# Two chained network blocks in one kernel: mixer ends worked off in batches, fused mask-and-maximum, and neighbourhood attention with its rotation, value transposes and bias mask placed inside its projections

## The chip, the cores and the metric

The kernel runs on one core of a Trainium2 chip. The metric is the device time of one execution in microseconds (us), here the median of three. Five engines work side by side, each through its own queue of instructions in order, and wait for one another on semaphores: PE (TensorE: matrix products, with PEld its weight loads), ACT (ScalarE), DVE (VectorE), POOL (GpSimd) and SP (SyncE, which here only issues DMAs). PSUM has eight banks of 512 fp32 values per partition.

## The reference, cut to what matters

A first block of two layers (half-step SwiGLU, a mixer, half-step SwiGLU, each with a post-norm modulated by "ada" vectors) over 256 latent and 256 context rows of width 1024. The mixer of its layer 0 is neighbourhood attention (NA), that of layer 1 a short convolution. A second block of two layers over 384 rows, of which the kernel carries 272; each layer has three mixers whose outputs are normalised per head, gated and summed:

```python
# NA (once): per head, 256 queries against 256 window keys and 256 context keys
q = apply_axial_rope(qkv[:, :, 0]); k = apply_axial_rope(qkv[:, :, 1])
s_win = where(mask, q @ k * scale + bias, -inf);  s_ctx = q @ k_c * scale
p = softmax(concatenate([s_win, s_ctx]))
out = p[..., :nk] @ v + p[..., nk:] @ v_c
# second block, per layer
o_ret = rms(retention(...)) * silu(gate)        # 4 heads of 256 columns
o_hg  = rms(hgrn2(...)) * silu(gate)            # 8 heads of 128
p = softmax(where(allowed, s, MASK_VALUE)); w = p[:, :, 0] - lam * p[:, :, 1]
o_da  = rms(w @ v) * subln_g * (1 - lambda_init) # 8 heads of 128, two score maps each
y = sum_n sigmoid(gate_n) * (branch_n @ w_branch_n)
```

## The kernel before

**GEMMs.** Everything is fp32. A weight product is made of three matrix products of reduced operands: high by high (line 1721), activation-low by weight-high (1722) and activation-high by weight-low (1723). The list `gemm_steps` gives the order of all projections. A step is worked in units of 256 output columns (two PSUM banks), a unit in chunks of K = 512: 24 matmuls per chunk. Per chunk SP fetches the raw weights (2 x 256 KB, line 1567), ACT casts them to `high` (line 1791) and DVE subtracts to get `low` (line 1969); raw, high and low have four slots. In the first block, chunks also host "ada" parts: 256 KB more of weights (L1572) and matmuls at line 1634.

**NA.** The steps are q (256 rows: 8 chunks), k and v (512 rows each: 8 chunks each), then the output projection "res". Between v's last matmul and the first scores `na_pe` transposes the values (L1377; ACT copies them, L1432), and rotates q and k: PE multiplies by a permutation (L1384), POOL multiplies by cosines (L1503), DVE by sines (L1468) and adds (L1471). DVE adds the column mask to the whole bias table `TB` (L1462) ahead of that. Then 32 units (16 heads x 2 query tiles, two units per step j) run as a pipeline: scores (PE, L1396); bias add, context copy, negated maximum (DVE, L1486, L1487, L1489); exponential with sum (ACT, L1447); reciprocal (DVE, L1478); scaling (POOL, L1506); transposes (PE, L1417); copy of them (ACT, L1443); values (PE, L1406). The score tiles `SB` are a ring of six. DVE waits for the transposes of unit t-6 before it writes unit t.

**Mixer ends.** In all three mixers of the second block (ret, hg and da; `out_bank`, `tail_act_square` to `tail_dve_low` at lines 630 to 687, and the same for hg at 1100 to 1186 and 1346 to 1356) a head's output stays in its PSUM bank through the whole chain: ACT squares it, PE sums the squares with a matrix of ones, ACT takes Ln and Exp(-0.5 x) of the sum, DVE scales and gates it out of PSUM, ACT casts, DVE subtracts. Ln and Exp are in different tables of ACT, so each alternation loads two tables. Two tiles of `SX`, `SY` and rdev alternate. The next matrix work in the program, the "mgate" step, has its first four chunks placed among the heads ("early" chunks, lines 1669 to 1671); the "branch" step follows. PE waits for the last scaled head (`s_ot`) before it goes on. In da 24 units (8 heads x 3 chunks of queries) are a pipeline over PE, DVE, ACT, with two maps each; DVE adds the mask (L986) and reduces to the maximum (L989).

The order of the work is the order in which the code of each engine is written; there is no scheduler.

## Time and profile before

| | us |
|---|---|
| median of 3 runs | 3321.48 (3318.24 to 3323.4) |
| the profiled execution's own time | 3321.1 |
| its span | 3319.3 |
| PE busy | 3015.6 (91%) |
| DVE busy | 1769.4 (53%) |
| ACT busy | 1427.5 (43%) |
| POOL busy | 431.8 (13%) |
| mean granted TensorE clock | 0.937 |

The profile is one execution. The time differs from the span by what lies outside it, 1.8 us. A matmul's busy time is modelled, so neighbouring ones overlap in the rows; the distance of their starts tells what one costs. A waiting engine appears as idle time before an instruction with the instruction that released it. Clock 1.00 is full speed; DMA share is the mean busy share of the 16 DMA engines.

### The profile page before, as it was taken

To read this page: it belongs to the slowest core of one execution; us is meant where nothing else is said; L and a number is where in the kernel's file an instruction comes from. 1 tells how busy PE (TensorE), PEld (TensorE's weight loads), DVE (VectorE), ACT (ScalarE), POOL (GpSimd) and SP (SyncE) were. 2 spreads that over 40 slices of the span, in tenths; PEclk is the share of its full clock that TensorE was granted. 3 is DMA by queue.
4 is the path that set the end of the run, shared out by engine and by line. 5 is a ranking of instruction groups with operands and counts; after the bars stand their busy time and mean duration, and the time that the engine had idled before them with its cause. 6 is when DMAs were issued, how large, how long until landed. Compare 5 with 4: busy or idle time off the path is not lost.

```text
span 3319.3 us, 53884 instructions
## 1 busy us (share of the span) xinstructions
PE 3015.6 (91%) x20792; PEld 2696.5 (81%) x20792; DVE 1769.4 (53%) x2514; ACT 1427.5 (43%) x1986; POOL 431.8 (13%) x330
## 2 busy tenths in 40 slices
PE   5999997977998989897999889889989987988898
PEld 2667765746998989897999778689988986967898
DVE  2323224375555556554547646658654574575684
ACT  1222113135445444544455443746535444355563
POOL 2111000052211101110100202001110020010110
PEclk7999998989999999998999879689999997978999
DMA  8885455601655645554445034045543530523453
GB/s 290 280 256 159 129 163 164 191 20 58 183 178 146 181 149 178 146 180 138 153 129 167 23 108 134 26 131 168 179 142 116 168 100 26 165 64 102 133 174 124
DMA packets 586160, 474.86 MB, mean 143 GB/s; under 512 B 28720, under 2 KB 547888, under 8 KB 585664
## 3 DMA queue, kind: packets, MB, share of 16 engines
q1 hardware_dynamic: 584464, 460.44, 45.2%
q0 software_dynamic: 1520, 11.95, 1.2%
q8 instruction: 125, 2.05, 0.3%
q14 instruction: 51, 0.42, 0.0%
HBM read 471.23 MB, written 4.72 MB: 143 GB/s over the span
## 4 chain that ended last, share of the span: by engine, by line
PE 83%; DVE 7%; ACT 4%; issue 3%; DMA 1%; SPq 1%; POOL 0%; DVEq 0%; ACTq 0%
PE PS L1721 24%; PE PS L1722 23%; PE PS L1723 23%; PE PS L1634 3%; PE PS L520 1%; PE PS L882 1%; PE PS L1108 1%; PE PS L870 1%; SPq L1572 1%; PE PS L1669 1%; PE PS L1670 1%; PE PS L1671 1%; ACT high L1791 1%; PE PS L718 1%; PE PS L1058 1%
## 5 line engine op out<-in xcount | busy, mean ns | idle before, releaser
L1969 DVE TENSOR_TENSOR low<-raw,high 128x1024 fp32r<-128x1024 f32 (+1 forms) x744 | 909.9, 1226 | 906.1 <-ACT high L1791 899.1
L1791 ACT CAST high<-raw 128x1024 fp32r<-128x1024 f32 (+1 forms) x744 | 767.6, 1033 | 1141.7 <-PE PS L1723 854.0
L1721 PE MATMUL PS<-NHh,high 128*128 128x272 f32 x2304 | 682.6, 296 | 65.7 <-issue 21.9
L1723 PE MATMUL PS<-NHh,low 128*128 128x272 f32 x2304 | 674.8, 293 | 0.0
L1722 PE MATMUL PS<-NHl,high 128*128 128x272 f32 x2304 | 673.3, 292 | 0.0
L1721 PE MATMUL PS<-XH,high 128*128 128x256 f32 (+1 forms) x1856 | 590.1, 318 | 51.8 <-DVE XL L2011 30.9
L1722 PE MATMUL PS<-XL,high 128*128 128x256 f32 (+1 forms) x1856 | 582.9, 314 | 0.0
L1723 PE MATMUL PS<-XH,low 128*128 128x256 f32 (+1 forms) x1856 | 582.2, 314 | 0.0
L1721 PEld LDWEIGHTS PS<-NHh,high 128*128 128x128 f32 x2304 | 443.4, 192 | 71.3 <-issue 54.1
L1721 PEld LDWEIGHTS PS<-XH,high 128*128 128x128 f32 x1856 | 360.5, 194 | 111.6 <-issue 91.1
L1722 PEld LDWEIGHTS PS<-NHl,high 128*128 128x128 f32 x2304 | 443.5, 193 | 0.8
L1723 PEld LDWEIGHTS PS<-NHh,low 128*128 128x128 f32 x2304 | 442.8, 192 | 0.0
L1723 PEld LDWEIGHTS PS<-XH,low 128*128 128x128 f32 x1856 | 360.4, 194 | 19.9
L1722 PEld LDWEIGHTS PS<-XL,high 128*128 128x128 f32 x1856 | 360.7, 194 | 17.5
L1721 PE MATMUL PS<-GH,high 128*128 128x256 f32 (+1 forms) x768 | 238.8, 311 | 0.8 <-POOL GL L2288 0.8
L1723 PE MATMUL PS<-GH,low 128*128 128x256 f32 (+1 forms) x768 | 236.2, 308 | 0.0
L1722 PE MATMUL PS<-GL,high 128*128 128x256 f32 (+1 forms) x768 | 236.1, 307 | 0.0
L2288 POOL TENSOR_TENSOR GL<-SG,GH 128x256 f32 (+1 forms) x92 | 122.0, 1327 | 728.7 <-ACT GH L1871 633.6
L1721 PEld LDWEIGHTS PS<-GH,high 128*128 128x128 f32 x768 | 146.7, 191 | 26.4 <-issue 20.3
L1723 PEld LDWEIGHTS PS<-GH,low 128*128 128x128 f32 x768 | 146.7, 191 | 7.2
L1722 PEld LDWEIGHTS PS<-GL,high 128*128 128x128 f32 x768 | 146.7, 191 | 6.2
L1834 ACT ACTIVATE SG<-PS 128x256 f32<-128x256 f32 (+1 forms) x88 | 38.4, 437 | 206.1 <-PE PS L1723 206.1
(293 smaller groups left out, 4235.4 us busy)
## 6 DMA issues: line engine op xcount, KB each, us to landing
raw<-w_in_dram SPq DMA_DIRECT2D x416, 256.0 KB, 3.0
raw<-ffn_w_in_dram SPq DMA_DIRECT2D x352, 256.0 KB, 3.2
part<-ada_w_dram SPq DMA_DIRECT2D x184, 256.0 KB, 4.1
raw<-w_ffn_in_dram SPq DMA_DIRECT2D x176, 256.0 KB, 3.2
raw<-ffn_w_out_dram SPq DMA_DIRECT2D x160, 256.0 KB, 3.1
raw<-w_branch_dram SPq DMA_DIRECT2D x96, 256.0 KB, 3.1
raw<-w_ffn_out_dram SPq DMA_DIRECT2D x80, 256.0 KB, 3.0
part_sg<-ada_w_dram SPq DMA_DIRECT2D x48, 256.0 KB, 3.0
```

The costliest lines, as they stand in the source:

```text
L520: last = nc.tensor.matmul(PS[:, b, 0:T], ones[:], src[:, k, 0:T], start=(k == 0), stop=(k == KT - 1))
L718: nc.tensor.matmul(PS[:, 6 + u % 2, 0:T2], rot, MI[:, u, :], start=True, stop=True).then_inc(s_rot, 1)
L870: last = nc.tensor.matmul(PS[0:wd, 2 * (t % 2) + m, 0:t0 + wd], MI[r, h, t0:t0 + wd], MI[r, 8 + h, 0:t0 + wd], start=True, stop=True)
L882: last = nc.tensor.matmul(PS[:, out_bank(2, h), t0:t0 + wd], VT[0:kw, c, h * P:(h + 1) * P], flat(MG[0:kw, 2 + 2 * (u % 2):4 + 2 * (u % 2) ...
L1634: last = nc.tensor.matmul(PS[32 * g:32 * g + 32, ROW_BANK + t % 2, :], SCW[:, k, SC0 - 2 * x:SC0 - 2 * x + 32], src[:, 2 * y:2 * y + 2, :] ...
L1721: nc.tensor.matmul(out, wh, xh, start=(k0 + k == 0), stop=False)
L1722: nc.tensor.matmul(out, wh, xl, start=False, stop=False)
L1723: last = nc.tensor.matmul(out, wl, xh, start=False, stop=(c == len(kch) - 1 and k == nk - 1))
L1791: nc.scalar.copy(high[:, slot, 0:nk, :], raw[:, slot, 0:nk, :]).then_inc(s_high, 1)
L1834: nc.scalar.activation(SG[:, p:p + 1, 0:T], bank(p, 0)[:, :, 0:T], ACT.Sigmoid).then_inc(s_act, 1)
L1969: nc.vector.tensor_tensor(low[:, slot, 0:nk, :], raw[:, slot, 0:nk, :], high[:, slot, 0:nk, :].bitcast(F32), ALU.subtract).then_inc(s_low, 1)
L2288: nc.gpsimd.tensor_tensor(out, x, h.bitcast(F32), ALU.subtract).then_inc(s_hl, 1)
```

## The change

1. **Order of the NA projections:** v, k, q. The rotation goes pair by pair of tiles behind chunk 0 of the units k1 to k3 and q0 to q3 (the eighth pair in `na_pe`); the value transposes go in eight halves behind chunk 1 of the units of k and q. They use banks 5 and 4 (`COL_BANK`, `SUM_BANK`). The bias mask goes to DVE behind k3 (12 heads) and q0 (4 heads), `hg_bounds` into the attention loop's end.
2. **NA loop:** the three DVE instructions become one `tensor_tensor_reduce` (minimum of bias minus score), with a tail of zeros behind `TB` for the context half and the exponential's scale turned to -1. Probabilities of odd units are scaled on DVE, of even ones on POOL.
3. **Mixer ends:** DVE gates each head out of PSUM into `EX` at once, ACT squares, PE writes the sums into banks that came free; Ln for half of the heads in one instruction, Exp likewise, then scaling (DVE), cast (ACT), low part (DVE) per pair. In da, ACT copies each head to `EX`, squares it and copies its sum, and Ln, Exp and what follows stand behind the last head. PE no longer waits for `s_ot`; the branch step waits for the low parts chunk by chunk.
4. **da:** mask and maximum become one `tensor_tensor_reduce` for each map.

```diff
+                add("v", 4, plain(w["na_w_qkv"][0], 2 * D), layer, T=T1)
+                add("k", 4, plain(w["na_w_qkv"][0], D), layer, T=T1)
+                steps[-1]["pairs"], steps[-1]["halves"] = {1: 0, 2: 1, 3: 2}, {u: u for u in range(4)}
                 add("q", 4, plain(w["na_w_qkv"][0], 0), layer)
-                add("k", 4, plain(w["na_w_qkv"][0], D), layer, T=T1)
-                add("v", 4, plain(w["na_w_qkv"][0], 2 * D), layer, T=T1)
+                steps[-1]["pairs"], steps[-1]["halves"] = {u: 3 + u for u in range(4)}, {u: 4 + u for u in range(4)}
...
+        def tail_logs(act, layer, n, half):
...
+                act.wait_ge(s_osum, DH * layer + 4 * half + 4)
+                src = head_rdev(2, half)
...
+                act.wait_ge(s_oms, tail_first(layer, n) + 2 * half + 2)
+                b, w_ = ((2, 0)[half], 2) if n == 0 else (4 * half, 4)
+                src = PS[:, b:b + w_, 0:T2]
+            nc.scalar.activation(head_rdev(n, half), src, ACT.Ln, bias=epsc[:, 0:1],
...
+        def tail_exps(act, layer, n, half):
+            act.wait_ge(s_oln, half_first(layer, n) + half + 1)
+            rs = head_rdev(n, half)
...
+        def tail_high(act, layer, n, v):
+            act.wait_ge(s_ot, pair_first(layer, n) + v + 1)
+            nc.scalar.copy(OH[:, 2 * v:2 * v + 2, :], EX[:, 2 * v:2 * v + 2, :]).then_inc(s_oth, 1)
...
+        def tail_scale(dve, layer, n, v):
+            dve.wait_ge(s_ord, half_first(layer, n) + v // 2 + 1)
...
+            def square_sum(h):
+                pe.wait_ge(s_osq, hh0 + h + 1)
+                ones_sum(PS[:, (2, 3, 0, 1)[h], 0:T2], MI[:, 8 + 2 * h:10 + 2 * h, :], 2).then_inc(s_oms, 1)
...
-            pe.wait_ge(s_ot, hh0 + 2)
...
+            pe.wait_ge(s_oln, half_first(layer, 0) + 2)
...
+                act.wait_ge(s_oev, evac_first(layer, 0) + h + 1)
+                b = ret_out_bank(h)
+                nc.scalar.activation(MI[:, 8 + 2 * h:10 + 2 * h, :], PS[:, b:b + 2, 0:T2],
+                                     ACT.Square).then_inc(s_osq, 1)
+            tail_logs(act, layer, 0, 0)
+            early_split(0)
+            tail_logs(act, layer, 0, 1)
+            tail_exps(act, layer, 0, 0)
+            tail_exps(act, layer, 0, 1)
+            early_split(1)
+            early_gate(0)
+            tail_high(act, layer, 0, 0)
+            early_split(2)
+            tail_high(act, layer, 0, 1)
+            tail_high(act, layer, 0, 2)
+            early_gate(1)
+            tail_high(act, layer, 0, 3)
+            early_split(3)
...
+                dve.wait_ge(s_o, hh0 + h + 1)
+                b = ret_out_bank(h)
+                nc.vector.tensor_tensor(EX[:, 2 * h:2 * h + 2, :], PS[:, b:b + 2, 0:T2],
+                                        MI[:, 16 + 2 * h:18 + 2 * h, :], ALU.mult).then_inc(s_oev, 1)
...
+                if t >= 7 and (t - 7) % 3 == 2:
+                    h = (t - 7) // 3
+                    act.wait_ge(s_o, hh0 + h + 1)
+                    nc.scalar.copy(EX[:, h, :], PS[:, 5 + h % 2, 0:T2])
+                    nc.scalar.activation(MI[:, 16 + h, :], PS[:, 5 + h % 2, 0:T2], ACT.Square).then_inc(s_osq, 1)
...
+                if t >= 8 and (t - 8) % 3 == 2:
+                    h = (t - 8) // 3
+                    act.wait_ge(s_oms, hh0 + h + 1)
+                    nc.scalar.copy(MI[:, 16 + h, :], PS[:, 7, 0:T2]).then_inc(s_osum, 1)
             early_split(3)
+            for half in range(2):
+                tail_logs(act, layer, 2, half)
+            for half in range(2):
+                tail_exps(act, layer, 2, half)
+            for v in range(4):
+                tail_high(act, layer, 2, v)
...
-                    mask = bc(con2[0:wd, C2["dmask"] + n * T2:C2["dmask"] + n * T2 + t0 + wd], 2)
-                    nc.vector.scalar_tensor_tensor(s, PS[0:wd, b:b + 2, 0:t0 + wd], 64 ** -0.5, mask,
-                                                   ALU.mult, ALU.add).then_inc(s_dm, 1)
-                    dve.wait_ge(s_dm, u0 + u + 1)
-                    nc.vector.tensor_reduce(dst[0:wd, u % 4, 0:2], s, AX.X, ALU.max, negate=True).then_inc(s_dx, 1)
-                if t >= 10 and (t - 10) % 3 == 2:
-                    tail_dve_low(dve, 2, hh0 + (t - 10) // 3, (t - 10) // 3)
-                if t >= 9 and (t - 9) % 3 == 2:
-                    tail_dve_gate(dve, link, 2, hh0 + (t - 9) // 3, (t - 9) // 3)
+                    mask = con2[0:wd, C2["dmask"] + n * T2:C2["dmask"] + n * T2 + t0 + wd]
+                    for m in range(2):
+                        last = nc.vector.tensor_tensor_reduce(s[:, m, :], PS[0:wd, b + m, 0:t0 + wd], mask,
+                                                              -(64 ** -0.5), -NEG, ALU.add, ALU.min,
+                                                              dst[0:wd, u % 4, m:m + 1])
+                    last.then_inc(s_dx, 1)
...
+            outs(0)
+            outs(1)
+            outs(2)
+            square_sums(0)
+            outs(3)
+            for v in range(1, 4):
+                square_sums(v)
+            pe.wait_ge(s_oln, half_first(layer, 1) + 1)
...
+            tail_logs(act, layer, 1, 0)
+            early_split(2)
+            tail_logs(act, layer, 1, 1)
+            tail_exps(act, layer, 1, 0)
+            tail_exps(act, layer, 1, 1)
+            early_split(3)
+            for v in range(4):
+                tail_high(act, layer, 1, v)
...
+        def na_rope_pe(pe, i):
...
+            pe.wait_ge(s_free, (k if i < 4 else q) + i % 4 + 3)
+            pe.wait_ge(s_mod, turns_done[0])
+            if i:
+                pe.wait_ge(s_nr1, i)
+            for x in range(2):
+                last = nc.tensor.matmul(PS[:, COL_BANK, x * SEQ:(x + 1) * SEQ], con1[:, C1["rot"]:C1["rot"] + P],
+                                        na_tiles(i)[:, x, :], start=True, stop=True)
+            last.then_inc(s_nrot, 1)
...
+        def na_values_pe(pe, h):
...
+            for f in range(4):
+                last = nc.tensor.transpose(PS[:, SUM_BANK, f * P:(f + 1) * P], NVT[:, 4 * a + f, n * P:(n + 1) * P],
+                                           ident)
+            last.then_inc(s_nvt, 1)
...
+        def na_rope_dve(dve, i):
...
+            dve.wait_ge(s_nrot, i + 1)
+            nc.vector.tensor_tensor(rot, PS[:, COL_BANK, :].rearrange("p (a t) -> p a t", a=2), sin,
+                                    ALU.mult).then_inc(s_nr1, 1)
+            dve.wait_ge(s_nr1, i + 1)
+            dve.wait_ge(s_nrc, i + 1)
+            nc.vector.tensor_tensor(x, x, rot, ALU.add).then_inc(s_nr2, 1)
...
+            na_rope_pe(pe, 7)
+            pe.wait_ge(s_nr2, KT)
+            pe.wait_ge(s_nvc, KT)
...
+            nc.vector.memset(TBZ[:, NH * 6 * GRID_W:], 0.0)
+            na_rope_dve(dve, 7)
...
+                    if u % 2:
+                        dve.wait_ge(s_nr, u + 1)
+                        nc.vector.tensor_scalar(sb(u), sb(u), nst[:, u % 6, 2:3], None, ALU.mult).then_inc(s_nwd, 1)
...
+                    b = TBZ[:, at:at + SEQ]
+                    b = bass.AP(b.tensor, b.offset, [b.ap[0], [NH * 6 * GRID_W - at, 2], [1, SEQ]])
...
-                    nc.vector.tensor_tensor(sb(t)[:, 0:SEQ], PS[:, bk, 0:SEQ], b, ALU.add)
-                    nc.vector.tensor_copy(sb(t)[:, SEQ:T1], PS[:, bk, SEQ:T1]).then_inc(s_na, 1)
-                    dve.wait_ge(s_na, t + 1)
-                    nc.vector.tensor_reduce(nst[:, t % 6, 0:1], sb(t), AX.X, ALU.max,
-                                            negate=True).then_inc(s_nm, 1)
+                    nc.vector.tensor_tensor_reduce(sb(t).rearrange("p (a n) -> p a n", a=2),
+                                                   PS[:, bk, :].rearrange("p (a n) -> p a n", a=2), b, -1.0, -NEG,
+                                                   ALU.add, ALU.min, nst[:, t % 6, 0:1]).then_inc(s_nm, 1)
+                if t == NU + 4:
+                    hg_bounds(dve, link)
...
+            cos = bc(con1[:, C1["cos"]:C1["cos"] + SEQ], 2)
+            for i in range(KT):
+                pool.wait_ge(s_nrot, i + 1)
+                nc.gpsimd.tensor_tensor(na_tiles(i), na_tiles(i), cos, ALU.mult).then_inc(s_nrc, 1)
+            for u in range(0, NU, 2):
...
+                if pairs_done[0]:
+                    pe.wait_ge(s_nr1, pairs_done[0])
...
-                if name == "branch":
-                    pe.wait_ge(s_tail_low, tail_count(s["layer"], s["n"]))
...
+                    if name == "branch":
+                        pe.wait_ge(s_tail_low, pair_first(s["layer"], s["n"]) + 2 * c + 2)
...
+                        if not rolled(s) and c == 0 and u in s.get("pairs", ()):
+                            na_rope_pe(pe, s["pairs"][u])
+                        if not rolled(s) and c == 1 and u in s.get("halves", ()):
+                            na_values_pe(pe, s["halves"][u])
...
-                    pe.wait_ge(s_ot, tail_count(s["layer"], s["mixer"]))
...
+                    if u in s.get("pairs", ()):
+                        na_rope_dve(dve, s["pairs"][u])
...
+                    if name == "k" and u == 3:
+                        na_bias_dve(dve, slice(0, 12))
+                    if name == "q" and u == 0:
+                        na_bias_dve(dve, slice(12, NH))```

ACT, end of the hg mixer. Before (L1172 squares, L1183 is Ln, L1186 is Exp, L1176 the cast):

```order
L1172 ACTIVATE SX<-PS 128x544 x2
L1183 ACT_TABLE_LOAD
L1183 ACTIVATE MJ<-PS,epsc 128x544
L1186 ACT_TABLE_LOAD
L1186 ACTIVATE MJ<-MJ 128x544
L1172 ACTIVATE SX<-PS 128x544
L1176 CAST OH<-SY 128x544
L1183 ACT_TABLE_LOAD
```

ACT at the same place now (L1854 is the weight cast of a chunk, L1210 squares, L670 is Ln, L676 is Exp, L680 the cast):

```order
L1854 CAST high<-raw 128x1024 x2
L1210 ACTIVATE QB<-PS 128x544 x4
L670 ACT_TABLE_LOAD
L670 ACTIVATE MJ<-PS,epsc 128x1088
L1854 CAST high<-raw 128x1024
L670 ACTIVATE MJ<-PS,epsc 128x1088
L676 ACT_TABLE_LOAD
L676 ACTIVATE MJ<-MJ 128x1088 x2
L1854 CAST high<-raw 128x1024
L680 CAST OH<-EX 128x544 x4
```

Squares now stand together, and the alternation of Ln and Exp has become one pass. In the whole program ACT has 64 table loads where it had 114.

DVE in the NA loop, two units of it before (SB is the score tile, nst the column of statistics):

```order
L1486 TENSOR_TENSOR SB<-PS,TB 128x256
L1487 COPY SB<-PS 128x256
L1489 TENSOR_REDUCE nst<-SB 128x1
L1478 RECIPROCAL nst<-nst 128x1
L1486 TENSOR_TENSOR SB<-PS,TB 128x256
L1487 COPY SB<-PS 128x256
L1489 TENSOR_REDUCE nst<-SB 128x1
L1478 RECIPROCAL nst<-nst 128x1
```

DVE in the same loop now (L1544 is the fused instruction, which stands as two; L1534 scales an odd unit):

```order
L1531 RECIPROCAL nst<-nst 128x1
L1534 TENSOR_SCALAR SB<-SB,nst 128x512
L1544 ISA SB,nst<-PS,TBZ 128x512
L1544 ISA nst 128x1
L1531 RECIPROCAL nst<-nst 128x1
```

Three instructions before the exponential are now two, and every other unit has a scaling ahead of the next unit's fused instruction.

PE between the last projection and the first scores, before:

```order
L1723 MATMUL PS<-XH,low 128x512
L1377 MATMUL PS<-con_54,NVT 128x128 x32
L1384 MATMUL PS<-NQ,con_54 128x256 x8
L1384 MATMUL PS<-NK,con_54 128x256 x8
L1396 MATMUL PS<-NK,NQ 128x512 x8
```

The same place now (L1423 is a value half, L1410 the rotation, L1465 the scores):

```order
L1784 MATMUL PS<-XH,low 128x256
L1423 MATMUL PS<-con_54,NVT 128x128 x4
L1410 MATMUL PS<-NQ,con_54 128x256 x2
L1465 MATMUL PS<-NK,NQ 128x512 x8
```

Of 48 instructions 6 are left there; the others stand behind chunks of k and q.

## Rows read from the trace of the kernel before

**Rows 1.** The page, part 4: the ending chain by engine

```profile
PE 83%; DVE 7%; ACT 4%; issue 3%; DMA 1%; SPq 1%; POOL 0%; DVEq 0%; ACTq 0%
```

**Rows 2.** Stretches: from:to length, busy PE PEld DVE ACT POOL, clock, DMA share, GB/s

```profile
527.80:572.50 44.70, 40.16 (x242) 31.52 (x243) 17.32 (x20) 14.97 (x17) 4.94 (x6) 0.91 0.77 212
572.50:672.90 100.40, 100.34 (x447) 71.31 (x446) 30.16 (x32) 16.78 (x16) 4.88 (x6) 1.00 0.63 189
1651.20:1686.80 35.60, 32.18 (x185) 27.45 (x186) 13.48 (x26) 22.40 (x29) 0.00 (x0) 0.95 0.08 25
1893.20:1939.20 46.00, 28.09 (x96) 22.10 (x96) 9.40 (x14) 21.52 (x25) 0.00 (x0) 0.51 0.07 23
2061.00:2151.00 90.00, 74.43 (x356) 49.89 (x357) 60.13 (x169) 67.30 (x182) 1.62 (x3) 0.67 0.06 18
2077.60:2112.20 34.60, 31.38 (x129) 18.47 (x129) 26.70 (x79) 29.51 (x84) 0.00 (x0) 0.60 0.00 1
```

**Rows 3.** Chain of waits in the q projection: start, us, what

```profile
546.17 7.58 DMA part_sg<-ada_w_dram
555.26 7.99 DMA part_sg<-ada_w_dram
```

**Rows 4.** Timeline at v's end: start, us, engine, line, operation [idle before <- releaser]

```profile
672.22 0.39 PE L1722 MATMUL PS<-XL,high 128*128 128x512 f32 x1
672.45 0.39 PE L1723 MATMUL PS<-XH,low 128*128 128x512 f32 x1
672.88 1.23 DVE L2103 COPY NVT<-PS 128x1024 f32<-128x1024 f32 x1 [3.08 <-PE PS L1723]
674.16 1.97 PE L1377 MATMUL PS<-con,NVT 128*128 128x128 f32 x16 [1.32 <-DVE NVT L2103]
675.63 6.55 DVE L1462 TENSOR_TENSOR TB<-TB,con 128x6144 f32<-128x6144 f32 x1
```

**Rows 5.** Groups by line, 676 to 700.2 us: busy, mean ns, idle before

```profile
L1503 POOL TENSOR_TENSOR NQ<-NQ,con 128x256 f32<-128x256 f32 x8 | 9.0, 1132 | 83.7 <-PE PS L1384 83.6
L1384 PE MATMUL PS<-NK,con 128*128 128x256 f32 x16 | 6.6, 527 | 2.0 <-DVE ROT L1468 2.0
```

**Rows 6.** Timeline at the first scores

```profile
700.30 2.93 PE L1396 MATMUL PS<-NK,NQ 64*128 64x512 f32 x6 [1.94 <-DVE NK L1471]
701.31 0.34 PEld L1396 LDWEIGHTS PS<-NK,NQ 64*128 64x128 f32 x2 [0.51 <-issue]
702.16 0.34 PEld L1396 LDWEIGHTS PS<-NK,NQ 64*128 64x128 f32 x2 [0.51 <-issue]
```

**Rows 7.** Timeline of one period of the NA loop

```profile
734.28 0.42 DVE L1486 TENSOR_TENSOR SB<-PS,TB 128x256 f32<-128x256 f32 x1 [1.32 <-PE PS L1417]
735.07 0.69 DVE L1489 TENSOR_REDUCE nst<-SB 128x1 f32<-128x512 f32 x1
735.79 0.72 ACT L1447 ACTIVATE SB<-SB,nst 128x512 f32<-128x512 f32 x1 [1.00 <-DVE nst L1489]
736.42 0.19 ACT L1447 ACTIVATION_READ_ACCUMULATOR SB<-SB,nst 128x1 f32 x1
738.92 0.42 DVE L1486 TENSOR_TENSOR SB<-PS,TB 128x256 f32<-128x256 f32 x1 [1.65 <-PE PS L1417]
```

**Rows 8.** Chain of waits, first matmul of the output projection

```profile
780.15 0.39 PE PS L1721
```

**Rows 9.** Chain of waits in the ret end, early chunks' matmuls

```profile
1672.81 0.23 PE PS L1669
1676.17 0.13 PE PS L1669
```

**Rows 10.** hg end, waits: us in total, times, longest

```profile
DVE SY L1355 <- ACT MJ L1186: 36.5, 4, 11.9
```

**Rows 11.** da, 2061 to 2151 us: groups of ACT by line

```profile
L657 ACT ACT_TABLE_LOAD x8 | 10.3, 1283 | 0.1
```

**Rows 12.** Timeline at the branch step behind da

```profile
2151.02 0.56 PE L1721 MATMUL PS<-NHh,high 128*128 128x272 f32 x1 [6.19 <-DVEq L2071]
```

More of the change, by code:

```diff
@@ L328, in two_block_kernel @@
         SB2 = Region(e1_at).take("SB2", [P, 2, T1])
-        ROT = A4.take("ROT", [P, 2, SEQ])
         nst = A4.take("nst", [P, 6, 4])
@@ L652, in tail_act_rdev, with ret_out_bank, hg_out_bank, head_rdev @@
-        def tail_act_rdev(act, n, hh, h):
-            act.wait_ge(s_oms, hh + 1)
-            if hh >= 2:
-                act.wait_ge(s_ot, hh - 1)
-            rs = RS[:, hh % 2, 0:T2]
-            nc.scalar.activation(rs, PS[:, 7, 0:T2], ACT.Ln, bias=epsc[:, 0:1],
+        def ret_out_bank(h):
+            return (2, 4, 0, 6)[h]
+        def hg_out_bank(v):
+            return 2 * v
+        def head_rdev(n, half):
+            if n == 0:
+                return MJ[:, 2 * half:2 * half + 2, :]
+            return (MJ[:, 0:8, :] if n == 1 else MI[:, 16:24, :])[:, 4 * half:4 * half + 4, :]
@@ L679, in tail_dve_gate @@
[L679 to L687 removed]
+                nc.vector.tensor_tensor(y, y, pair_rdev(n, v), ALU.mult).then_inc(s_ot, 1)
@@ L909, in da_act @@
             u0, hh0 = DU * layer, tail_first(layer, 2)
-            for t in range(DU + 9):
+            for t in range(DU + 8):
                 if 5 <= t < DU + 5:
@@ new lines, in outs @@
+            def outs(v):
+                if v == 3:
+                    pe.wait_ge(s_free, U_end + 4)
+                for h in (2 * v, 2 * v + 1):
+                    f = slice(h * P, (h + 1) * P)
+                    for n, (t0, wd) in enumerate(CHUNKS):
+                        out = PS[:, hg_out_bank(v) + h % 2, t0:t0 + wd]
+                        last = nc.tensor.matmul(out, VT[0:wd, n, f], AM[0:wd, h, t0:t0 + wd], start=True,
+                                                stop=(n == 0))
+                        if n:
+                            last = nc.tensor.matmul(out, ST[:, n - 1, f], Q_[:, h, t0:t0 + wd], start=False,
+                                                    stop=True)
+                last.then_inc(s_o, 1)
@@ new lines, in square_sums @@
+            def square_sums(v):
+                pe.wait_ge(s_osq, u0 + v + 1)
+                for x in range(2):
+                    last = nc.tensor.matmul(PS[:, hg_out_bank(v) + x, 0:T2], ones[:], QB[:, 2 * v + x, :],
+                                            start=True, stop=True)
+                last.then_inc(s_oms, 1)
+            outs(0)
[5 more added lines that the diff above has]
+                square_sums(v)
@@ L1370, in na_pe, with na_bias_dve @@
+        def na_bias_dve(dve, heads):
+            dve.wait_ge(s_bias, 16 * 12)
+            tb = TB[:, heads, :, :].rearrange("p h j c -> p (h j) c")
+            colmask = con1[:, C1["colmask"]:C1["colmask"] + GRID_W]
+            nc.vector.tensor_tensor(tb, tb, bc(colmask, 6 * (heads.stop - heads.start)), ALU.add)
         def na_pe(pe, U_end):
@@ L1429, in na_act @@
         def na_act(act):
-            for n in range(4):
-                act.wait_ge(s_nvt, n + 1)
-                nc.scalar.copy(NV[:, n, :].rearrange("p (a t) -> p a t", a=2),
-                               PS[:, 2 * (n % 2):2 * (n % 2) + 2, :]).then_inc(s_nvc, 1)
             act.wait_ge(s_lb, 1)
@@ L1446, in na_act @@
                     act.wait_ge(s_nm, u + 1)
-                    nc.scalar.activation(sb(u), sb(u), ACT.Exp, bias=nst[:, u % 6, 0:1],
+                    nc.scalar.activation(sb(u), sb(u), ACT.Exp, bias=nst[:, u % 6, 0:1], scale=-1.0,
                                          accum_out=nst[:, u % 6, 1:2]).then_inc(s_ne, 1)
@@ L1901, in after @@
                         values_act(act, s, u)
-                behind(act, s, split_high, epilogue, second, between, after if "at" in s else None)
+                    if "halves" in s:
+                        na_values_act(act, s["halves"][u])
+                behind(act, s, split_high, epilogue, second, between, after if "at" in s or "halves" in s else None)
                 if name == "conv":
```

324 lines of the change are left out of this document (116 added, 208 removed).

## The prediction

> **What bounds the kernel now.** I read the chain that ended last first: 83% of it is PE [rows 1], mostly weight matmuls that the change leaves alone. So a gain can only come where PE idles, waits or runs at a low clock. I then cut the trace into stretches around the edits and read PE busy, clock and DMA share of each. The reader should see four places. The q projection takes 44.70 us for half the columns of k or v, with PE busy 40.16, and its chain runs through ada weight transfers of 7.58 and 7.99 us [rows 2, 3]. From the end of v to the first scores, and then through the attention loop, PE waits for others [rows 4 to 8]. The ends of the mixers have PE idle 3.4 (ret), 17.9 (hg) and 15.6 us (da), the last two at a granted clock of 0.51 and 0.67 [rows 2]. Layer 1 of the second block repeats these three stretches to within 0.1 us, so each mixer term counts twice.
>
> **NA projections.** k and v: 100.34 us for 16 chunks is 6.27 per chunk, of which 24 matmuls of 512 columns, 0.23 from start to start [rows 4], make 5.43 and an ada part 0.84. q has half the columns: 2.72 + 0.84 = 3.56 per chunk, 28.5 for eight, some 29.7 with its own column matmuls. It takes 44.7: 15 us of excess. In v first, a chunk of 6.27 us hides a transfer that a chunk of 3.56 does not; in q last the four slots are full when it begins. About 4 of the 15 are the low clock behind a long wait (clock 0.91 in the stretch [rows 2]), which v now pays; I recover 11. If the transfers also hold up q in its new place, none of it comes: bounds 0 and 15.
>
> Added inside PE's stream: 32 value transposes, at 1.97 us for 16 [rows 4] that is 3.9; 14 rotation matmuls. A full fp32 matmul of 512 columns is 0.85 (the pairs of loads at 701.31 and 702.16, [rows 6]), so 256 columns are about 0.45, 6.3 in all; above, 6.6/8 = 0.83 each [rows 5]. Fifteen interruptions of the stream, each between 0.05 (from the end of the copy at 672.88 + 1.23 to the transposes at 674.16 [rows 4]) and 0.51 (the idle weight loader between two L1396 loads [rows 6]), taken as 0.2: 3.0. Four chunks of q that host two ada parts: 1.5 of waiting. Together 14.7, against the 11: v's end 672.7 becomes 676.4 for the last projection matmul.
>
> What is left before the scores: evacuation 0.7, last low rotation pair and its sin, cosine, add in series (PE 0.9, POOL 1.4, DVE 0.7 + 0.7) and DVE's small operations ahead of it, 1.2 + 0.7: 6.3 us. Before, this gap was 27.6 us (672.7 to 700.30 [rows 4, 6]), with the mask add of 6.55 first [rows 4] and then 16 dependent rotations. First score 682.7: **17.6 us saved**. Bounds: 7 (no transfer recovered) and 22.
>
> The mask add, now 4.9 and 1.6 us on DVE, sits behind k3 and q0 while DVE has a cast's subtraction to do per chunk; DVE is busy 30.16 of 100.4 us there [rows 2], so it has cover; were the cover gone, PE would wait once for at most 4.9. POOL's cosine products share those chunks with DVE's subtractions. In the first eight products POOL took 1.132 us on average, against 0.734 for the next eight in the same window, the first of them beside the 6.55 us mask add [rows 4, 5]. The Trainium skill, "SBUF — State Buffer", section on the shared port pair, says that a DVE operation with two SBUF inputs and a GpSimd one lock each other out for a whole instruction. By that rule each of 7 pairs may cost DVE up to 1.4 us; the row agrees with a delay of POOL, and the sum stays as it is since neither is bound there.
>
> **NA loop.** First score to output projection: 780.15 - 700.30 = 79.85 us [rows 6, 8]. A period of two units is 738.92 - 734.28 = 4.64 [rows 7]. Its loop is: bias, copy, maximum until the exponential starts, 1.51 (735.79 - 734.28); exponential and accumulator read 0.73; copy 0.6; values 1.03; transposes until DVE may write the slot again 0.76. The fused instruction does 512 columns; the reduction over the same 512 takes 0.69 [rows 7]. Then comes the accumulator read, 0.15 to 0.19 as ACT's [rows 7]. So 1.51 becomes 0.90: 0.61 per period, 12 periods, 7.3. The six units of start-up, now 1.44 each on DVE, and the wait for twelve small DVE operations (701 to 702.5), which move to the end: 2.9. Last units: 0.6. **10.9 us saved.** Below: if the fused operation takes 0.53 more (one more pass of 512), each period gains 0.08 and this term falls to 1. Above: 14. DVE has per period, with one odd scaling, about 2.5 of 4.0 us, ACT 3.1, PE 3, POOL 1.6: none takes over.
>
> **ret ends.** PE idles 35.6 - 32.18 = 3.4 us [rows 2], and 18 matmuls of the early chunks run 0.10 us slower than the others (0.23 against 0.13 [rows 9]), 1.8, which goes if PE does not pause ahead of them. I take **4.9** of 5.2 per layer; bounds 0 and 5.2.
>
> **hg ends.** DVE waits 36.5 us in four waits for the Exp of a pair [rows 10], since squares, sums, Ln and Exp of one pair follow one another through a bank that stays occupied. Afterwards outs of all pairs run without that; eight table loads become two, of 1.28 us each by the same kind's row in da [rows 11]. What stays is PE's own 28.09 of 46.0 us, if the clock stays 0.51 [rows 2]. About 0.9 remains before PE may go on behind the last sum (gate 0.74, square 0.62, beside two other sums; then Ln). **17.0** per layer; bounds 12 and 31, the latter if the clock doubles.
>
> **da.** Four heads take 34.60 us, 8.65 a head: PE busy 31.38, ACT 29.51, DVE 26.70 [rows 2]. Per head two table loads of 1.283 [rows 11], Ln 0.49, Exp 0.43 and cast 0.42 leave ACT, two copies (0.40 and 0.35) come: 7.4 - 3.9 + 0.75 = 4.2. DVE gets rid of gate and low part (0.92) and of about a third of mask and maximum: 5.5. PE has 7.85 at clock 0.60, 4.7 at full clock. The head then takes between 7.85 and 5.5; I take 7.2, nearer to the low clock. 1.45 for 5.7 heads with two tails in them, 8.2; start 1.5; end 4.5, where PE now idles 6.19 before the branch step [rows 12] and 1.2 go by low clock, less 3 that come: ACT does Ln, Exp and casts of all heads (9.7 us) ahead of the mgate step's casts. **14.2** per layer of the 15.6 idle plus clock; bounds 5 and 23.
>
> **Sum.** Per layer 4.9 + 17.0 + 14.2 = 36.1, twice 72.2; NA 17.6 + 10.9 = 28.5; 100.7 together. The profiled execution took 3321.1, 0.4 below the median of 3321.48. 3321.1 - 100.7 = **3220 us**.
>
> **Rivals.**
> *The fused operation runs at half rate.* For it: it reads two tensors and keeps a running minimum. Against: the reduction of 512 and the two-input subtraction of 1024 (1.22 us) both pass about one column per ns. At 0.53 more for 512 and 0.27 for 256 columns the NA term loses 10 and da 9: 3240. The Trainium skill, "Vector Engine (DVE) Microarchitecture Reference", "Points that are easy to get wrong", says that such an operation with two non-bf16 sources in SBUF runs at half throughput. Here one source is in PSUM, so by its words the rule does not apply; were it to, the time is this rival's.
> *da stays bound by PE at the low clock.* The clock in the steady window is 0.60, with PE busy 91% of it [rows 2]. If it stays, a head takes 7.85 or more, and what is saved at the end turns into ACT's batch. Two layers give 19 less: 3239.
> *PE gets full clock in the tails.* In ret the clock is 0.95 with PE hardly idle, in hg 0.51 with 39% idle [rows 2]. Without the idle stretches hg's matmuls may take half, and da's heads 6.0: another 2 x 10 and 2 x 8: 3184.
> *Slower: each fused operation has a fixed price.* ACT pays 1.283 us whenever its function changes [rows 11]. Should DVE pay something alike for an instruction of a new kind, 32 + 96 = 128 of them stand on the path of NA and da. From 0.8 us each they eat all 100.7; at 1.283 they cost 164: 3384. Against: no such time shows before any DVE instruction in these rows.
>
> **How the numbers follow.** Forecast 58%; half rate 13%; da at PE's low clock 10%; full clock 12%; fixed price 5%; no net change within 0.2% (6.6 us, about what three runs can tell) 2%, by several terms failing at once. The likeliest alone is 3220, from 3203 to 3237. The range leaves out the fixed price and the far half of the full-clock case: 3180 to 3258, which also holds the case that no transfer time comes back in q (3231) with half rate on top (3250). Faster 0.93, same 0.02, slower 0.05.
>
> **What would show it.** The gap from the last projection matmul to the first score at 6 us, q's chunks near 3.6 us; the NA period at 4.0 us with an exponential some 0.9 after the fused instruction's start; in hg, PE without gaps above 1 us; in ret 31 us; da's heads at 7.2. Wrong it is if the fused instruction has over 1.2 us for 512 columns, if q's chunks still wait for transfers in the new place, or if the branch step waits over 5 us behind da for ACT's batch.

## The result, and the profile after

| | before | after |
|---|---|---|
| median, us | 3321.24 (3318.24 to 3323.4) | 3236.43 (3235.52 to 3239.61) |
| profiled execution, its span | 3321.1, 3319.3 | 3239.61, 3237.7 |
| ratio | | 0.9749 (0.9733 to 0.9764) |
| mean granted clock of PE | 0.937 | 0.951 |

The kernel takes 84.8 us less; the forecast was 100.7 less (3220), with a range of 3180 to 3258. The two profiled executions differ by 81.6 us in the span (the one after is the slowest of its four). Cut at the same instructions of PE, this is where the us went:

| stretch | forecast, us less | measured, us less |
|---|---|---|
| v, k, q: first projection matmul to the first score | 17.6 | 5.4 |
| NA loop, first score to output projection | 10.9 | 11.7 |
| ret ends, both layers (ret's first score to hg's first output) | 9.8 | 11.5 |
| hg ends, both (hg's first output to da's first score) | 34.0 | 39.2 |
| da, both (da's first score to the next layer or the end) | 28.4 | 14.4 |
| elsewhere, where nothing was changed | 0 | -0.7 |

The last row is 3.0 us more ahead of the first projection matmul (it stands at 527.9 us before and at 530.9 after; in the other traces it lies between 527.6 and 532.8) and 2.3 less between the output projection and ret.

Stretches after, in layer 0, with busy PE, PEld, DVE, ACT, POOL, then clock, DMA share, GB/s; they answer to [rows 2], [rows 6] and [rows 8]. They are the second half of the projections, the NA loop, the ret end, the hg end and da from its first to its last score:

```profile
650.00:690.60 40.60, 34.59 (x228) 28.51 (x227) 21.85 (x22) 8.67 (x11) 7.94 (x4) 0.92 0.61 194
697.90:766.05 68.15, 53.25 (x449) 32.91 (x449) 37.24 (x131) 44.25 (x104) 25.11 (x16) 0.96 0.00 1
1634.80:1665.50 30.70, 30.68 (x189) 26.66 (x190) 13.84 (x26) 14.60 (x20) 0.00 (x0) 1.00 0.19 62
1871.90:1898.50 26.60, 26.60 (x101) 22.80 (x102) 6.22 (x7) 6.28 (x8) 0.00 (x0) 0.55 0.13 40
2021.60:2076.40 54.80, 50.12 (x210) 28.67 (x209) 33.47 (x174) 29.46 (x125) 0.79 (x2) 0.59 0.02 7
```

The reader should see four kinds. In ret PE now has no gap and the full clock. In hg it has no gap either, once the outputs have begun, but a clock of 0.55. In da (first to last score) PE is busy 50.12 of 54.80 at 0.59, while DVE and ACT are busy 61% and 54%. And in most of q (650 to 690.6) PE idles 6 us and the clock is under 1. One period of the loop, DVE and ACT, which answers to [rows 7]:

```profile
726.15 0.69 DVE L1544 CUSTOM_DVE_ANT_1 SB<-PS,TBZ 128x512 f32<-128x512 f32 x1 [1.58 <-PE PS L1486]
726.77 0.08 DVE L1544 DVE_READ_ACCUMULATOR2_ANT nst<- 128x1 f32 x1
726.89 0.72 ACT L1512 ACTIVATE SB<-SB,nst 128x512 f32<-128x512 f32 x1 [0.25 <-DVE nst L1544]
730.04 0.69 DVE L1544 CUSTOM_DVE_ANT_1 SB<-PS,TBZ 128x512 f32<-128x512 f32 x1 [1.92 <-PE PS L1486]
```

The fused operation takes 0.69 us for 512 columns, as the plain maximum did. The exponential begins 0.74 us behind its start (1.51 before), and the period is 3.89 us (4.64 before, 4.0 forecast).

Where q loses its time, chosen rows of PE, DVE and ACT from the timeline, in order:

```profile
669.83 1.05 ACT L1854 CAST high<-raw 128x1024 fp32r<-128x1024 f32 x1 [7.12 <-DMA raw<-na_w_qkv_dram]
670.91 1.23 DVE L2034 TENSOR_TENSOR low<-raw,high 128x1024 fp32r<-128x1024 f32 x1 [4.86 <-ACT high L1854]
672.05 0.68 DVE L1438 TENSOR_TENSOR RS<-PS,con 128x512 f32<-128x512 f32 x1
672.88 1.10 PE L1410 MATMUL PS<-NQ,con 128*128 128x256 f32 x4 [1.38 <-DVE RS L1438]
676.94 1.04 ACT L1854 CAST high<-raw 128x1024 fp32r<-128x1024 f32 x1 [4.30 <-PE PS L1784]
678.01 1.22 DVE L2034 TENSOR_TENSOR low<-raw,high 128x1024 fp32r<-128x1024 f32 x1 [0.44 <-ACT high L1854]
679.16 0.68 DVE L1438 TENSOR_TENSOR RS<-PS,con 128x512 f32<-128x512 f32 x1
679.99 1.85 PE L1707 MATMUL PS<-con,adarow 128*128 128x8 f32 x8 [2.70 <-DVE RS L1438]
693.62 2.04 PE L1410 MATMUL PS<-NQ,con 128*128 128x256 f32 x4 [2.70 <-DVE RS L1438]
```

Read it upwards from PE's waits of 1.38, 2.70 and 2.70 us. Each time PE wants to issue the next rotation or the ada columns, which need DVE's sine product of the pair before (L1438). That product's own input had long been there, but in DVE's queue it stands behind the evacuation of the unit and the weight subtraction behind that (L2034), and the subtraction waits for ACT's cast. What the cast waits for differs. Ahead of the first wait it is a weight transfer (7.12 us). Ahead of the second, and of the third with a cast at 690.57, it is PE itself (4.30 and 2.69 us): the cast takes a slot that PE frees with the last chunk of the unit. So in these two cases no transfer is late; PE stands still while cast, subtraction and product follow one another, because the product was written behind them. Behind the second wait the clock falls: it is 0.50 from 682 to 686, where matmuls of 256 columns start every 0.21 us instead of 0.12.

### The profile page after: what moved, and what is told of

It reads as the page before. It is cut to its first block and busy times, and to the rows that moved or that the text cites. A ratio compares the mean times of both kernels' runs of the same rounds, so it can differ in the third digit from the quotient of the medians.

```text
span 3237.7 us, 53764 instructions
## 1 busy us (share of the span) xinstructions
PE 2994.8 (92%) x20792; PEld 2684.8 (83%) x20792; DVE 1727.0 (53%) x2564; ACT 1360.7 (42%) x1924; POOL 406.3 (13%) x306
## 5 line engine op out<-in xcount | busy, mean ns | idle before, releaser
L2034 DVE TENSOR_TENSOR low<-raw,high 128x1024 fp32r<-128x1024 f32 (+1 forms) x744 | 912.3, 1229 | 894.3 <-ACT high L1854 886.3
L1854 ACT CAST high<-raw 128x1024 fp32r<-128x1024 f32 (+1 forms) x744 | 767.6, 1033 | 1128.3 <-PE PS L1784 833.6
L1782 PE MATMUL PS<-NHh,high 128*128 128x272 f32 x2304 | 679.0, 295 | 39.5 <-issue 21.9
L1784 PE MATMUL PS<-NHh,low 128*128 128x272 f32 x2304 | 671.7, 292 | 0.0
L1782 PE MATMUL PS<-XH,high 128*128 128x256 f32 (+1 forms) x1856 | 590.9, 318 | 49.6 <-DVE XL L2076 28.7
L1784 PE MATMUL PS<-XH,low 128*128 128x256 f32 (+1 forms) x1856 | 582.1, 314 | 0.0
L1782 PEld LDWEIGHTS PS<-NHh,high 128*128 128x128 f32 x2304 | 439.7, 191 | 43.5 <-issue 40.9
L1782 PEld LDWEIGHTS PS<-XH,high 128*128 128x128 f32 x1856 | 360.0, 194 | 101.4 <-issue 82.1
L1784 PEld LDWEIGHTS PS<-NHh,low 128*128 128x128 f32 x2304 | 439.1, 191 | 0.0
L1784 PEld LDWEIGHTS PS<-XH,low 128*128 128x128 f32 x1856 | 359.9, 194 | 20.1
L1782 PE MATMUL PS<-GH,high 128*128 128x256 f32 (+1 forms) x768 | 238.8, 311 | 0.8 <-POOL GL L2359 0.8
L1784 PE MATMUL PS<-GH,low 128*128 128x256 f32 (+1 forms) x768 | 236.2, 308 | 0.0
L1782 PEld LDWEIGHTS PS<-GH,high 128*128 128x128 f32 x768 | 146.6, 191 | 26.4 <-issue 20.3
L1784 PEld LDWEIGHTS PS<-GH,low 128*128 128x128 f32 x768 | 146.7, 191 | 7.3
L2251 DVE TENSOR_TENSOR SG<-SG,PS 128x256 f32<-128x256 f32 (+1 forms) x88 | 42.9, 487 | 157.7 <-ACT SG L1897 157.7
```

What stands on the lines that cost most here:

```text
L1782: nc.tensor.matmul(out, wh, xh, start=(k0 + k == 0), stop=False)
L1784: last = nc.tensor.matmul(out, wl, xh, start=False, stop=(c == len(kch) - 1 and k == nk - 1))
L1854: nc.scalar.copy(high[:, slot, 0:nk, :], raw[:, slot, 0:nk, :]).then_inc(s_high, 1)
L2034: nc.vector.tensor_tensor(low[:, slot, 0:nk, :], raw[:, slot, 0:nk, :], high[:, slot, 0:nk, :].bitcast(F32), ALU.subtract).then_inc(s_low, 1)
L2251: nc.vector.tensor_tensor(sg, sg, bank(p, 0)[:, :, 0:T], ALU.mult).then_inc(s_mid, 1)
```

## The experiments

Times are medians, each set with its own runs of the kernel before. The whole change is 84.8 less in the first comparison and 82.1 less in e9.

### Halves of the change: e1, e2

e1 keeps NA as it was (parts 1 and 2 of the change left out), e2 the mixer ends and da (parts 3 and 4 left out).

> Only the mixer ends and the fused mask and maximum of da are changed; all of neighbourhood attention is as in the kernel before. Theory A (the two parts are independent, and the anchors of the two traces split the gain rightly): attention gave 14.1 us of the 84.8, so this takes 3250 to 3254 us. Rival B (part of the 70 us seen behind attention is an after-effect of it, as transfers that start earlier or the clock): over 3256 us.

> Only neighbourhood attention is changed (order v, k, q, insertions, fused loop), the mixer ends are as before. Theory A: 14 to 16 us less than before, 3305 to 3307 us. Rival B: the sum of the two halves misses the whole by more than 3 us.

e1: 3248.83 us (before 3319.51, ratio 0.9799, 0.9778 to 0.9819), 70.7 less. e2: 3301.21 (0.9942, 0.9925 to 0.9959), 18.3 less. Both came out better than by Theory A, and their sum, 89.0 against 84.8, misses the whole by more than the 3 us that e2's rival B had set, by a little. Two things bear on it. Both expectations took NA's projections at 2.4 us, a difference of two positions counted from the start of the execution; from the first projection matmul on it is 5.4 (the table above), which with the loop's 11.7 makes 17.1. And in the profiled execution of e1 most of the surplus is in one place: in its layer 1 the hg end runs at the full clock by itself, and from hg's first output to da takes 140.2 us, not 149.3 as after. The stretch, and how it begins:

```profile
2728.20:2752.00 23.80, 22.67 (x155) 20.51 (x156) 8.28 (x10) 12.40 (x14) 0.00 (x0) 1.00 0.21 67
2728.22 0.71 PE L1140 MATMUL PS<-AM,VT 128*128 128x128 f32 x4 [2.33 <-DVE MI L1367]
```

Its outputs span 11.8 us there, and 19.5 us in its layer 0 and in layer 1 of the changed kernel. The same instructions, behind the same wait of 2.33 us, go either way: the clock there is at an edge, and e8 asks what tips it.

### The projections: e3, e10, e4

e3 puts the old order and the old block between projections and scores back; e10 has the new order with that old block. In both, `hg_bounds`, which stood in the old block and now stands at the loop's end, is worked twice: eleven small DVE operations too many (e10's loop takes 69.4 us, e3's 68.3, after 68.2). The diff of e10, cut:

```diff
-                steps[-1]["pairs"], steps[-1]["halves"] = ...   # both
-            na_rope_pe(pe, 7)
+            ...   # 32 transposes, then 16 rotations, as before
```

> As the changed kernel, but the projections are in the old order q, k, v, and rotation, value transposes and bias mask stand between them and the scores as before; the fused loop stays. Theory A (the insertions into the projections gained only 2.4 us, the loop 11.7): 3238 to 3240 us. Rival B (the prediction's term of 17.6 us for the projections was right and something else lost it): 3252 us or more.

> As the changed kernel, with the order v, k, q, but rotation, value transposes and bias mask all between the last projection matmul and the scores, as before. Theory J (the order alone lets q's transfers be hidden, by what is left of q's excess behind its first 8.4 us, some 6; the insertions then cost about what they save): 3236 to 3241 us, the last projection matmul 5 to 7 us nearer to the first one than before. Rival K (q is held by transfers in either place): 3243 to 3247 us, as with the old order.

e3: 3244.85 (3241.0 to 3247.7; ratio 0.9777, 0.9761 to 0.9794). That is neither Theory A (3238 to 3240) nor Rival B (3252 or more): insertions and order together are worth 8.4 us by the medians, more than the 2.4 of the expectation. The traces below show 2.5 to 4 of them (the profiled execution of e3 is its fastest); the rest is not located. e10: 3246.39 (0.977, 0.9756 to 0.9785), beside e9, the changed kernel again:

> The changed kernel again, unaltered, on the chip of this call, so that the other three can be read against it: 3234 to 3239 us by every theory.

e9: 3238.89 us. So e10 is 7.5 slower than the changed kernel, and no faster than e3. In the traces, from the first projection matmul to the start of the last evacuation, then to the first score, us:

| | projections | gap | sum |
|---|---|---|---|
| before | 145.0 | 27.4 | 172.4 |
| e3 (same code here as before) | 142.0 | 27.5 | 169.5 |
| e10, order alone | 145.4 | 28.0 | 173.5 |
| after; e9 | 159.7; 159.0 | 7.3; 7.4 | 167.0; 166.4 |

The same code varies by some 3 us from one execution to the next: the sum is 168.8 in e1, with the code of before, and lies between 164.5 and 167.0 in all eight traces with the code of after. On average that is 170.2 against 165.9, some 4 us for part 1 of the change.

Rival K holds: the order alone recovers nothing, q still takes 37.2 us (636.35 to 673.53) for its eight chunks. In the trace of e10 PE waits there for ada transfers four times (0.21, 0.99, 0.91 and 0.89 us); one of them:

```profile
653.86 1.05 PE L1666 MATMUL PS<-part,SCW 128*32 128x512 f32 x4 [0.91 <-DMA part<-ada_w_dram]
```

The insertions cost 14 us in the stream and save 20.7 in the gap.

e4 moves DVE's rotation work (cut):

```diff
+                def roped(u, p):
+                    if mine: na_rope_dve(dve, pair)      # the sine product
+                    epilogue(u, p)
+                    if mine: na_rope_add(dve, pair)
-                    if u in s.get("pairs", ()):          # in after(u), behind the split
-                        na_rope_dve(dve, s["pairs"][u])
```

> As the changed kernel, but DVE multiplies a pair by the sines ahead of the unit's evacuation and adds right behind it, ahead of the next weight subtraction instead of behind it. Theory A (PE's three waits of 1.4, 2.7 and 2.7 us in q are a wait for DVE, which is held by a subtraction that waits for ACT's cast and that for a weight transfer, and the low clock follows from them): 5 to 9 us less than the changed kernel, 3228 to 3231 us, last projection matmul some 7 us earlier. Rival B (in the new place q is held by its transfers; the waits only sit where those show): under 2 us less, 3234 to 3237 us.

e4: 3229.11 (3224.63 to 3235.11; ratio 0.9733, 0.9717 to 0.9749). Projections 151.2 us, gap 5.6, first score after 156.7 instead of 167.0; 2.2 us are given back in the loop (70.4 against 68.2), and 8 remain at ret's start. In e12, which has the same edit, the two together take 157.4. Of PE's 6.8 us of waiting for the sine product (1.38, 2.70 and 2.70) nothing is left; all its waits from 645 to 684 us:

```profile
PE PS L1696 <- DMA part<-ada_w_dram: 1.8, 2, 1.0
PE PS L1410 <- DVE NQ L2170: 0.6, 1, 0.6
```

Theory A holds in that the product stood behind work that waits. Its last link, the weight transfer, holds for the first of the three waits only; in the other two the cast waited for PE (above). Of the 10.3 us, 6.2 are waits that are gone (6.8, less PE's new wait of 0.6). The 20 matmuls at low clock behind the second one, 0.09 us slower each, are 1.9 more; the rest was not traced. This rests on the traces; the medians of e4 and of the changed kernel are from different sets of runs, with ratios to before whose intervals meet.

### da: e5, e6, e11

```diff
+                    nc.scalar.copy(RS[:, 0, 0:T2], con2[:, 0:T2])   # e5, per head, behind the square
+                    nc.scalar.copy(RS[:, 1, 0:T2], con2[:, 0:T2])
```

> As the changed kernel, with two more copies of 272 columns on ACT in each head of da, behind the head's square: some 0.8 us of ACT more per head, 6.4 per layer. Theory C (in da PE at its low clock sets the period of a head): within 2 us of the changed kernel, 3235 to 3238 us, and the stretch from the first score of da to the next step grows by under 1 us. Rival D (ACT and its order in the loop still set the period): up to 12 us more, 3245 to 3249 us.

e5: 3238.54 (0.976, 0.9743 to 0.9776). From da's first score to the next layer's ret it takes 456.0 us, 455.7 in the changed kernel: 6.4 us of ACT cost 0.3. In layer 1, from da's first score to the end, it is 378.7 against 375.6, but 2.7 of these 3.1 us stand behind the branch step's first matmul, in code that the edit leaves alone, at a clock of 0.94 instead of 0.96. First to last score takes no longer in either layer (54.6 and 54.4, against 54.8 and 55.8). So ACT doesn't set the period of a head, which is Theory C; the time is 0.5 above its range.

e6 brings the two DVE instructions back in da (part 4 of the change undone).

> As the changed kernel, with mask and maximum in da as the two instructions of before; the tail stays batched. Theory C: no more than 2 us slower, since DVE has room beside PE. Rival D (the chain through DVE counts in each unit): 0.1 to 0.2 us for each of 48 units, 5 to 9 us slower, 3241 to 3246 us.

e6: 3242.94 (0.9773, 0.9756 to 0.9789), in the range of rival D, with 459.3 and 378.7 us for the two stretches, 3.6 and 3.1 more. But da itself accounts for little of it. From its first score to the branch step it takes 1.0 us more in layer 0 and 0.4 in layer 1; the other 2.6 and 2.7 stand behind, again in unchanged code, at a clock of 0.95 and 0.94 instead of 0.96, as in layer 1 of e5, whose DVE does nothing more. So the kernel is 6.5 us slower without the fusion in da, and 1.4 of them are the way through DVE: PE's next scores wait for the released bank. Whether the edit brings about the lower clock behind it is not shown. PE's wait for DVE in front of the scores of layer 0, e6 (L890) and then after (L889), us in total, times, longest:

```profile
PE PS L890 <- DVE MJ L1019: 3.9, 5, 1.7
```

```profile
PE PS L889 <- DVE dst L1019: 2.2, 3, 1.3
```

e11 gives PE more to do:

```diff
+                    for _ in range(4):
+                        nc.tensor.matmul(PS[:, 2 * (t % 2), 0:240], NHh[:, 0, 0:P], NHh[:, 0, 0:240],
+                                         start=True, stop=True)
                     for m in range(2):   # the scores of unit t, which overwrite it
```

> As the changed kernel, with four more f32r matmuls of 240 columns in front of the scores of each unit of da, written to the score bank and overwritten by the scores (their result is used nowhere). Theory L (a head's period in da hangs on PE's lower clock, and denser work on PE lifts the clock): the clock in da rises to 0.9 or more and the kernel gets faster although PE does more, 10 to 24 us less, 3213 to 3227 us. Rival M (the clock stays): 96 matmuls of 0.2 us per layer are added to a PE that is busy throughout, 19 us per layer, up to 38 us more, 3255 to 3275 us.

e11: 3214.53 us (before 3321.01, ratio 0.9675, 0.9662 to 0.9688), against 3238.89 for e9 beside it: 24.4 us faster with 192 matmuls more. From the first added matmul to about the last score, in both layers:

```profile
2019.10:2067.00 47.90, 45.03 (x302) 32.72 (x301) 33.86 (x174) 28.78 (x124) 1.35 (x2) 0.97 0.03 11
2849.60:2896.40 46.80, 43.78 (x303) 31.70 (x301) 34.27 (x176) 28.72 (x125) 1.48 (x2) 1.00 0.04 12
```

The clock is 0.97 and 1.00 where it was 0.59 and 0.61, and first to last score takes 47.0 and 46.5 us where it took 54.8 and 55.8. To the branch step it is 11.0 and 11.2 us less, nearly all of the 24.4. That is Theory L: PE at the low one of its two clock levels held da.

### Behind da: e7

```diff
+                    if h == 4:                    # ACT, inside the loop
+                        tail_logs(act, layer, 2, 0); tail_exps(act, layer, 2, 0)
+                    if h == 5:
+                        tail_high(act, layer, 2, 0); tail_high(act, layer, 2, 1)
```

DVE scales these pairs at t = 26 and subtracts at t = 28; heads 4 to 7 stay behind the loop.

> As the changed kernel, with Ln, Exp and casts of da's heads 0 to 3 inside the loop (behind heads 4 and 5) and only those of heads 4 to 7 behind it; it costs two table loads more per layer. Theory E (the 7.6 us that PE waits behind da in front of and inside the branch step come from ACT working off the batch ahead of the next weight casts): 2 to 3.5 us less per layer, 3229 to 3233 us. Rival F (those waits come from the transfers or from DVE): no gain, or 2 us more for the table loads.

e7: 3228.55 (before 3317.8; 0.9731, 0.9715 to 0.9747); from da to the next ret 452.1 us, 3.6 less. In the changed kernel the profile had, between 2090 and 2125 us,

```profile
PEld PS L1782 <- DVE low L2034: 3.9, 1, 3.9
PE PS L1782 <- DVEq L2203: 3.7, 1, 3.7
```

and neither is in e7. These two lines are one pause: the weight load at 2116.30 and its matmul at 2116.33 both stood still, so PE waited 3.7 us there and not 7.6, as the expectation has it by adding them. Layer 1 has the same pause. The 3.6 us of layer 0 are this wait. That is Theory E, a little above its upper end in time; in layer 1 the stretch is 7.1 us shorter, and the scores alone took 50.8 us, 55.8 in the changed kernel. The same edit left the scores of layer 0 at 54.8, and without it they took 52.5 in layer 1 of e4, so that part is again the clock (0.72 there in e7, 0.67 in e4 and 0.61 in the changed kernel).

### hg's clock: e8

```diff
-            early(2); early(3)                    # ahead of the transposes
 ...
+            early(2); early(3)                    # behind the state products
             pe.wait_ge(s_hd, d + HDV)
             pe.wait_ge(s_hp, p + HPO)
```

> As the changed kernel, with the early chunks 2 and 3 of hg's mgate placed behind the state products, right ahead of the outputs, where PE waited 2.3 us for DVE, instead of ahead of the transposes. Theory G (the granted clock of 0.5 in hg's end follows from PE's pauses ahead of it, as in ret, where the early chunks run through and the clock is 1.00): the outputs and sums run at the full clock, 26.6 us become about 15, 15 to 25 us less in all, 3212 to 3222 us. Rival H (the clock is low by the kind of matmuls in this stretch): 0 to 4 us less, by the wait covered.

e8: 3225.08 (0.9721, 0.9705 to 0.9737). The outputs span 11.7 us in both layers instead of 19.7 and 19.5; from hg's first output to da it takes 142.1 and 140.1 instead of 149.7 and 149.3. Both stretches are at clock 1.00, that of layer 0:

```profile
1870.10:1895.00 24.90, 23.79 (x167) 21.63 (x166) 9.59 (x12) 14.89 (x17) 0.00 (x0) 1.00 0.20 64
```

Theory G is right on the clock; the gain, 11.4 us, is smaller than it said. From ret's first score to hg's first output the kernel now takes 1.0 and 2.6 us more, since PE now waits 2.1 and 3.7 us ahead of the transposes, where the chunks stood. What e8 shows is that with two chunks right ahead of the outputs, and no wait there, the clock stays at 1.00 (four stretches of four, with e12). It does not show that the wait of 2.33 us alone brings it down: of the twenty hg ends with this wait, in the ten traces that have the new hg end without e8's edit, nineteen ran at 0.55 or 0.56 and one, layer 1 of e1, at 1.00. What made that one differ stays open.

### Together: e12

The edits of e4, e7 and e8 in one kernel.

> The changed kernel with the three edits that helped, together: sines and add of the rotation ahead of the weight subtraction, half of da's logs inside its loop, hg's early chunks 2 and 3 right ahead of its outputs. If their gains add: 7 + 7 + 11 us less than the changed kernel, 3209 to 3214 us. If they share a cause (the clock or the transfers behind them): 3215 to 3222 us.

e12: **3209.07 us** (3208.28 to 3214.58; ratio to before 0.9661, 0.9647 to 0.9674), 29.8 less than e9: the gains add (7.3, 7.9 and 11.4 by the medians above). It is the fastest kernel here. Its da is still at clock 0.56 and 0.60; e11's filler on top of it was not run.

## Why the prediction was right or wrong, point by point

- **Result.** Right in sign and inside the range; 16 us too optimistic at the centre. Two steps carry that, the projections and da.
- **"q ... 15 us of excess; I recover 11": wrong.** Two errors. The stretch [rows 2] was ended at q's last evacuation at 572.5, but DVE's evacuation stood behind a subtraction; PE's last matmul of q was at 567.1, and the stretch already held 5 us of k (so that k and v came out too short as well, and an undisturbed chunk of q too: from 564.28 to 568.33 it is 4.05 us and not 3.56). And the remaining excess was booked as movable. Recovered by the order: nothing (e10). The lower bound of the text, 0, was the truth, and so was its sentence on transfers that hold q in the new place, one of its signs of being wrong. The whole term is 5.4 and not 17.6.
- **"Added inside PE's stream ... 14.7": right in the sum, by luck.** 159.0 - 145.4 = 13.6 (e9, e10). But the items are others: 4.1 us of it, in the changed kernel's trace, are two waits for DVE, with a third of 2.70 in the gap, where the text had 3.0 for fifteen short interruptions. The step that failed: it priced the DVE work by its duration ("it has cover"), not by what stands ahead of it in DVE's order. e4 takes most of it back. The delay by POOL's products that it named was real for DVE too: DVE's subtraction of 1024 columns took 2.31, 2.17 and 2.15 us (at 651.95, 662.74 and 687.92) behind the start of such a product, instead of 1.22. None of PE's three waits hangs on these.
- **"What is left before the scores: 6.3": 7.3**, of which 2.7 is that wait. With e4 it is 5.6.
- **NA loop, 10.9: right, 11.7.** The accumulator read is 0.08 us and not 0.15 to 0.19. Half rate and a fixed price per fused instruction are both out: 0.69 us for 512 columns (0.37 on average over da's three sizes). The premise of the latter was too wide as well: in the lists above ACT goes from casts to squares without a table load.
- **ret, 4.9 per layer: right, 4.9 and 6.6.** In layer 1 more than the 5.2 of its upper bound; why was not traced.
- **hg, 17.0 per layer: 19.4 and 19.8.** PE does run its outputs without gaps at 0.55, as forecast. The end wait of 0.9 us did not appear in layer 0; in layer 1 PE waits 1.11 us for ACT's logarithm (L670). The full clock of the upper bound is real; e8 brings it about, and layer 1 of e1 had it without.
- **da, 14.2 per layer: wrong in size, 6.9 and 7.5.** The step: "I take 7.2" us a head. First to last score took 54.8 and 55.8 us, where it was 57.6: some 0.3 us a head less and not 1.45. The last four heads' starts lie 33.3 and 33.9 us apart, where it was 34.6. The rival "da stays bound by PE at the low clock" is what happened, and it should have been the likeliest: [rows 2] had PE 91% busy at 0.60. The end was forecast right: from the last score to the branch step 4.5 and 5.8 us less, forecast 4.5, with a wait of 3.7 us in front of the branch step where the text allowed 3. So the term missed by its heads, and the 1.5 of its start, alone.
- The two errors of 12.2 and 14.0 are partly offset by hg (5.2), ret (1.7) and the loop (0.8); 0.7 more is lost elsewhere.

## What to carry to other kernels

An instruction that is moved onto another engine's queue costs what it waits behind there: put work that another engine needs soon ahead of work that may have to wait, for a transfer or for that very engine, as e4 does. When PE is near 100% busy, read the clock before counting idle time as gain; a denser PE can be worth more than a shorter one (e8, e11). End a stretch at the instruction of the engine that you count, not at another engine's row for the same unit, and begin it at one too: 3 us of difference ahead of a stretch are not its own. A weight load and its matmul that stand still together are one wait. When an edit costs time, look where: in e5 and e6 most of it stood in code that was not edited.

## What the runs showed of the hardware that was not expected

- 96 additional f32r matmuls of 240 columns per layer, of no use to the result, made the kernel 24.4 us faster (e11), since in da PE was granted 0.97 and 1.00 in place of 0.59 and 0.61 (levels 2.4 and 1.2 GHz; the fraction is the mix of both).
- The same instructions at hg's end took 19.5 us in one layer and 11.8 in the other of one execution (e1), at clocks of 0.56 and 1.00, both times behind 2.33 us of idling. With two chunks of matmuls there instead, it was 1.00 four times of four (e8, e12); with the idling it was so once in twenty.
- DVE's fused tensor-tensor-reduce with one PSUM and one SBUF source ran at the speed of the plain maximum, 0.69 us for 512 columns, and its accumulator read took 0.08 us (changed kernel).
- Where POOL had begun a product of two SBUF inputs first, DVE's subtraction of 1024 columns took 2.15 to 2.31 us (at 651.95, 662.74 and 687.92); where the subtraction had begun first (673.98), it took 1.21 and the product 2.28 instead of 1.3 (changed kernel).
